# Two stages of a two-block kernel rearranged: the setup with the condition vector first, and the second input projection run together with the lead of the second attention

## The reference, cut to what matters

```python
def first_block(x, c, w_ada, b_ada, ...):
    mod = silu(c) @ w_ada + b_ada                  # six vectors of 1024
    h = rms_norm(x, pre_mix_g) * (1 + sc1) + sh1
    y = token_mixer(h, ...)                        # mLSTM heads and windowed attention, then w_out
    ...                                            # then the conv FFN

def second_block(x, norm1_g, w_in, ...):
    q, k, v, u = split(rmsnorm(x, norm1_g) @ w_in) # 512, 128, 128, 512 columns
    a = attention_mixer(q, k, v)                   # head norm, rope, full attention: 8 heads, 2 key heads
    p = pool_mixer(u)                              # 4 groups: windowed mean minus u, times pool_w, bias, scale
    x = x + concat([a, p]) @ w_out
    ...                                            # then the gated FFN
```

## Time and profile before

| | us |
|---|---|
| median of 3 runs (lowest, highest) | 2560.7 (2559.79, 2563.22) |
| the profiled execution, its own time | 2565.24 |
| its span in the trace | 2563.3 |
| TensorE busy in it | 2409.8 |
| VectorE, ScalarE, GpSimd busy | 1266.6, 832.0, 339.0 |

### The profile page before, as it was taken

The page is one execution under the profiler, slowest core; times in us unless marked ns, Lnnn a source line. Parts: engine busy times, 40 slices in busy tenths (PEclk is TensorE's granted clock), DMA queues, the critical chain, the costliest instruction groups (busy, mean ns, idle before and its releaser), DMA issues. The chain is left out here.

```text
span 2563.3 us, 28634 instructions
## 1 busy us (share of the span) xinstructions
PE 2409.8 (94%) x10895; PEld 1944.7 (76%) x10895; DVE 1266.6 (49%) x1537; ACT 832.0 (32%) x1247; POOL 339.0 (13%) x259
## 2 busy tenths in 40 slices
PE   5999965899999999999998969999999999999998
PEld 4788864677788888888876737777788888888887
DVE  5467246636644444444447359994423333333333
ACT  4232134834422222222235347873321111111111
POOL 1120012413100000000013606651000000000000
PEclk8999987999999999999999989999999999999999
DMA  8146421132211111111123230003111111111111
GB/s 315 57 134 201 143 79 62 33 115 80 60 50 43 48 49 49 49 49 49 50 99 120 58 90 20 22 9 115 34 50 50 49 49 49 49 49 49 49 48 67
DMA packets 188860, 181.92 MB, mean 71 GB/s; under 512 B 8349, under 2 KB 166893, under 8 KB 188145
## 3 DMA queue, kind: packets, MB, share of 16 engines
q1 hardware_dynamic: 185648, 173.36, 21.3%
q0 software_dynamic: 2176, 7.36, 0.9%
q10 hardware_dynamic: 961, 0.18, 0.0%
HBM read 152.55 MB, written 28.33 MB: 71 GB/s over the span
## 5 line engine op out<-in xcount | busy, mean ns | idle before, releaser
L289 PE MATMUL ps<-hhi,whi 128*128 128x512 f32 x1760 | 690.8, 393 | 2.7 <-DVE wlo L215 2.0
L291 PE MATMUL ps<-hhi,wlo 128*128 128x512 f32 x1760 | 686.4, 390 | 0.0
L290 PE MATMUL ps<-hlo,whi 128*128 128x512 f32 x1760 | 686.3, 390 | 0.0
L215 DVE TENSOR_TENSOR wlo<-raw,whi 128x1024 fp32r<-128x1024 f32 x178 | 229.8, 1293 | 369.0 <-ACT whi L210 369.0
L289 PEld LDWEIGHTS ps<-hhi,whi 128*128 128x128 f32 x1760 | 331.5, 188 | 74.3 <-DVE wlo L215 2.4
L290 PEld LDWEIGHTS ps<-hlo,whi 128*128 128x128 f32 x1760 | 331.5, 188 | 70.5 <-issue 1.9
L291 PEld LDWEIGHTS ps<-hhi,wlo 128*128 128x128 f32 x1760 | 331.4, 188 | 69.3
L210 ACT ACTIVATE whi<-raw 128x1024 fp32r<-128x1024 f32 x178 | 184.5, 1049 | 388.0 <-PE ps L2246 286.8
L2397 DVE TENSOR_TENSOR arena<-arena,ps 128x1024 f32<-128x1024 f32 x160 | 195.2, 1220 | 141.1 <-PE ps L2246 140.2
L2244 PE MATMUL ps<-hid_hi,whi 128*128 128x512 f32 x640 | 250.0, 391 | 0.0
L2245 PE MATMUL ps<-hid_lo,whi 128*128 128x512 f32 x640 | 249.2, 389 | 0.0
(11 more groups left out here) (318 smaller groups left out, 3206.7 us busy)
## 6 DMA issues: line engine op xcount, KB each, us to landing
raw<-in_w_up SPq DMA_DIRECT2D x66, 512.0 KB, 3.7
raw<-in_w_down SPq DMA_DIRECT2D x44, 512.0 KB, 3.5
raw<-in_w_in SPq DMA_DIRECT2D x32, 512.0 KB, 5.0
arena<-in_w_ada SPq DMA_DIRECT2D x32, 512.0 KB, 4.7
raw<-in_w_gate SPq DMA_DIRECT2D x22, 512.0 KB, 3.7
raw<-in_w_out SPq DMA_DIRECT2D x16, 512.0 KB, 3.6
arena<-x_park SPq DMA_DIRECT2D x2, 4096.0 KB, 12.2
x_park<-arena SPq DMA_DIRECT2D x4, 2048.0 KB, 8.9
```

What stands on the lines that cost most here:

```text
L215: nc.vector.tensor_tensor(wlo[:, w.off % RING, :], raw[:, w.off % RAW, :], whi[:, w.off % RING, :].bitcast(F32), ALU.subtract).then_inc(lo ...
L289: nc.tensor.matmul(acc[:, tok], whi[:, s, ws], hhi[:, k, tok], start=(k == 0), stop=False)
L290: nc.tensor.matmul(acc[:, tok], whi[:, s, ws], hlo[:, k, tok], start=False, stop=False)
L291: mm = nc.tensor.matmul(acc[:, tok], wlo[:, s, ws], hhi[:, k, tok], start=False, stop=(k == DK - 1))
```

## The change

It has three parts, in one diff.

**Setup.** The condition vector c is loaded by the first DMA of SyncE, and transposed, turned into `csil` before the other parameters are there. The row slots are 13: two of `cbuf`, seven of `chunk_work`, four of the unused halves of `whi` and `wlo`. All 16 rows are queued before the first two weight tiles; the seven small DMAs and the gate columns go behind those, on SyncE. The transposes of x come ahead of those of the parameters. ScalarE loads the table for logarithm and exponential in the setup, and makes the root of x there, beside the second reduction. The split of the gate columns moves behind the operands of the first product.

```diff
-        ada_slots = [cbuf[:, i, :] for i in range(4)] + [chunk_work[:, i * D:(i + 1) * D] for i in range(7)]
+        ada_slots = [cbuf[:, i, :] for i in range(2)] + [chunk_work[:, i * D:(i + 1) * D] for i in range(7)]
+        ada_slots += [v[:, i * D:(i + 1) * D] for v in (row_hi, row_lo) for i in (2, 3)]
...
+                sp.dma_start(c_in, a["c"].rearrange("a (j p) -> (a j) p", p=P)).then_inc(s_c, 16)
...
+                for n in range(ADA_FIRST * DK):
+                    if n >= len(ada_slots):
+                        sp.wait_ge(ada_added, n - len(ada_slots) + 1)
+                    ada_load(n)
+                for w in range(RAW):
+                    load(sp, At(w), tile_source(At(w)))
...
+                for w in range(AHEAD):
+                    split_hi(act, At(w))
+                act.wait_ge(x_summed, 1)
+                norm_mix.act_rstd(act, 0)
```

```diff
-                                mm = nc.tensor.matmul(acc[:, ks], q[:, h // 2, h % 2, :], klo[:, g, ks], start=False,
+                                mm = nc.tensor.matmul(acc[:, ks], q[0:64, h // 2, h % 2, :], klo[0:64, g, ks], start=False,
...
-                                mm = nc.tensor.matmul(o_, v[:, 64:192], ptls[g][:, k, :], start=False,
+                                mm = nc.tensor.matmul(o_[0:64, :], v[:, 64:128], ptls[g][:, k, :], start=False,
...
+                        lead.dve(dve)
                         maxima(At(0), 0)
+                        lead.dve_second(dve)
                         maxima(At(0), 1)
```

```diff
+        def product_by_tiles(pe, acc, w, between, passed=None):
...
+            for k in range(DK):
+                if k in between:
+                    between[k]()
...
+                        between = {2: lambda n=n: self.head_sums(pe, n), 6: lambda n=n: self.rotate(pe, n)}
+                        if t == 9:
+                            between[7] = lambda: self.keys.pe(pe)
...
+            def dve_unit(self, dve, e):
+                if e == 1:
+                    self.rope(dve, 4)
+                if e == 3:
+                    self.query_lo(dve, 3)
...
+            def act_unit(self, act, e):
+                if e == 0:
+                    act.wait_ge(q_lo, 3)
+                    act.wait_ge(q_stored[2], 64)
+                if e == 2:
+                    self.query_hi(act, 3)
+                if e == 4:
+                    act.wait_ge(pooling.mean, 4)
+                    act.wait_ge(q_stored[3], 64)
...
+            def sp_query(self, sp, j):
+
+                if j == 3:
+                    self.store(sp, j)
+                sp.wait_ge(q_stored[j], 64)
...
-                pair_products(pe, w, self.op_lo, u0)
+                pair_products(pe, w, self.op_lo, u0, lambda pe: pooling.pe(pe, range(2)), lambda pe: pooling.pe(pe, range(2, 4)))
```

More of the change, by code:

```diff
@@ L1458, in attention @@
             per_n = 2 * units
[L1459 removed]
+            names = ["keys", "klo", "vturned", "vhi", "vlo", "scores", "stat", "neg_max", "exp", "recip", "scaled",
                      "turned", "p_hi", "p_lo", "pv", "out"]
@@ L1639, in ahead @@
                     def ahead():
-                        nc.scalar.preload_act_table_set(EXP if full else LN_EXP)
+                        lead.act(act)
                         exponentials(At(0), 0)
@@ L1644, in body @@
                         for e in range(per_n):
+                            if full and n.off == 0 and n.i is None:
+                                lead.act_unit(act, e)
                             if e + 1 < per_n or more:
@@ L1698, in body @@
                                                     ALU.mult).then_inc(S["scaled"], 1)
+                            if full and n.off == 0 and n.i is None:
+                                lead.pool_unit(pool, e)
                         if not full and more:
@@ L1852, in body @@
                         for e in range(per_n):
+                            if full and n.off == 0 and n.i is None:
+                                lead.dve_unit(dve, e)
                             if e + 1 < per_n or more:
@@ L2574, in pe, with sums @@
-            def pe(self, pe):
-                for g in range(4):
-                    pe.wait_ge(self.mean, g + 1)
+                        self.link(pool, nc.gpsimd.memset(padded[g][:, side:side + 8], 0.0))
+            def sums(self, pool, g, n):
+                one, two = padded[4], padded[g]
+                pool.wait_ge(self.given, n)
+                if n > 1:
+                    pool.wait_ge(self.mean, n - 1)
+                cur, nxt, span = padded[g], one, PADT
+                for lv in range(g + 1):
+                    d = 1 << lv
+                    span -= d
+                    self.link(pool, nc.gpsimd.tensor_tensor(nxt[:, 0:span], cur[:, 0:span], cur[:, d:d + span], ALU.add))
+                    cur, nxt = nxt, (two if nxt is one else one)
+                return cur[:, 8 - (1 << g):8 - (1 << g) + T], nxt[:, 0:T - 16]
@@ L2577, in pe, with mean_of, difference @@
+            def mean_of(self, pool, g, s, mean):
+                self.link(pool, nc.gpsimd.tensor_scalar(mean, s[:, 8:T - 8], 1.0 / (2 << g), 0.0, ALU.mult, ALU.add))
+            def difference(self, pool, g, mean):
+                u = pool_u[:, g, :]
+                nc.gpsimd.tensor_tensor(u[:, 8:T - 8], mean, u[:, 8:T - 8], ALU.subtract).then_inc(self.mean, 1)
+            def pe(self, pe, gs):
+                for g in gs:
+                    pe.wait_ge(self.mean, 4)
                     if g >= 2:
@@ L2771, in block_kernel, with act @@
-        attention("attn2", True, stage=in2_stage)
+            def act(self, act, g):
+                act.wait_ge(self.product, g + 1)
+                nc.scalar.activation(pool_u[:, g, :], down[g % 2][:, :], ACT.Identity, bias=coef[:, 32 + g:33 + g],
+                                     scale=par_col("pool_scale_2", g)).then_inc(self.biased, 1)
+        pooling = Pooling()
+        ROPED2 = (0, 5, 6, 7, 8)
+        POOLED2 = (2, 3, 4, 9)
+        q_stored = [sem(f"query_stored{j}") for j in range(4)]
@@ L2774, in block_kernel @@
+        attention("attn2", True, SecondInput)
         class Operands:
```

848 lines of the change are left out of this document (427 added, 421 removed).

## The result

The changed kernel takes **2599.7 us** in the median (2596.3 to 2603.5) beside 2560.2 for the kernel before: a ratio of 1.0147, 95% interval 1.0132 to 1.0161. It is 39 us slower, where 30 us were to be gained. The profiled execution took 2602.1 us, its span 2600.3.

The account below looks back on a forecast made before the run. TensorE was busy 94% of the span, so gains could come only where it stands still; VectorE limits the steady full attention. 8.0 + 10.0 + 19.0 − 7.1 = 29.9 us gave 2531 us, range 2521 to 2541.

Parts of the forecast that it names:

- Setup: Start of the kernel: first product at 46.6 instead of 54.66, a gain of 8.0 us, bounds 5.5 and 10.0.
- The mishap of the lower bound: Setup: small DMAs and gate columns hold tile loads, or half clock falls on more square sums; gain only 5.5 us.
- First attention's lead: First attention: queries fetched earlier, so scores start 10.8 us earlier; taken as 10.0 us gain, bounds 8 and 11.5.
- Second projection and attention: Second input projection and full attention: first scaling 29.7 us earlier, part given back; gain 19.0 us, bounds 14 and 23.
- The fourth query: Full attention's first units: its fetch arrives at 1529.1, TensorE wants it at 1525.1; clock restarts cost some 2 us.
- rival 2: Second projection becomes a chain: late norm and root cost 3 us in each of four tiles, 2543 us; chance 0.17.
- Pooling products: Four products move into the second output projection, where TensorE is the bound: 7.1 us paid, bounds 5 and 8.
- the rival with the half-height matmuls: Attentions: height changes not overlapped, 0.17 us each, losing 35 us and up to 28, about 2590; chance 0.07.
- the change of width above: Trace row where width goes from 128 to 64 columns, spacing staying 0.22 us; cited against the half-height rival.

Follow-up runs that it names:

- the kernel with both mends: The changed kernel with low-key matmuls at 128 partitions again in both attentions and the parked x fetched back tile by tile: 2530.8 us, ratio 0.9870.
- the run with half-height products: The kernel before with 84 low-weight matmuls in six tiles of the second input projection cut to 64 partitions: 2599.2 us, ratio 1.0145.
- the kernel before with half height alone: The kernel before with only the low-key matmuls of both attentions cut to 64 partitions: 2621.6 us, ratio 1.0227.

## Why the prediction was wrong

The four terms of the sum held in size; the stages of the kernel with both mends show them without the two disturbances. What failed is what the sum left out.

**Setup**, 8.0: 8.75. The chain came as told, with errors that in part cancel: the third round of transposes stands at 17.9 (forecast 17.0), because x is waited for until 14.8 and not 13; from there to the second reduction it is 20.7 us, not the same 22.6, because the first sums of squares run at the full clock now (1.9 us for four passes, 3.7 before); the first operand operation stands at 41.98 (42.7), the first product at 45.91 (46.6). The mishap of the lower bound did not happen.

**First attention's lead**, 10.0: 10.8 in the mended kernel. The first scores follow the start of the key copies by 5.6 us in the changed kernel (412.12), where it was 16.45: the 10.8 us that the forecast began from. What came behind was slower.

**Second projection and attention**, 19.0: 17.9. The last product's end was put 139.7 us behind the projection's first (1501.1 less 1361.42); in the changed kernel the first scores stood at 1506.4, 139.1 behind. The first scaling came 145.2 us behind (1512.55), forecast 146.1. The fourth query, 4 us and 2 for the clock in the sum, costs 3.2 together. The projection did not become a chain (rival 2): no wait shows inside the tiles t = 6 to 9.

**Pooling products**, 7.1: twice 3.59 us, and the stage grew by 7.7.

The number failed in two places. **First, the rival with the half-height matmuls was priced rightly and given a chance of 0.07, and the sum put them at nothing.** The opening sentence on the long rows of products "that the change leaves as they are" does not hold for the attention, whose matmuls the change reshapes. The rival's 0.7 us per unit is what the timeline shows. Its 35 us for the full attention stand beside 29.8 us lost there; the rows give TensorE 11.5 us free over 56 units, 0.2 each and not 0.15, which makes 32. In the first attention the count was off: a unit has four half-height matmuls, so 8 changes and not 16, and 16 x 8 x 0.17 is 22 us. 24.6 were lost, and these are two things: at full clock a unit takes 5.2 us for 4.1 in the mended kernel, 17 us over 16 units, and the clock, at 0.50 when the scores begin at 412, comes back at 437 in the changed kernel (TensorE waits for nothing in between) and at 417 in the mended one. While it is at 0.50 a change costs more: the starts of a unit's scores lie 0.72 us apart near 1520, where neighbours of one height lie 0.43 apart, so 0.29 us. The rival's 2590 lies only 10 us under the result, and that is in part luck: the doubled count stands in for the late fetch, which it did not have.

The step that failed is the one that set the chance: "Against it: the change of width above". A row that shows a change of width says nothing on one of height; the two turned out opposite. The rule of the Trainium skill (TensorEngine Tiling (Array Packing), section Key Properties), that a change of tiling mode drains the engine, was set aside on that row alone. The runs agree with it for the height, at 0.205 us a change, and not for the width, at 0.005 or less. Rows with a change of height were there, if far from this case: at the gates (L948 and L951, 4 partitions) the loader stands for 0.76 us and then starts together with its matmul, at 153.26. They could not have settled it, because their neighbours are float32 matmuls of four passes, behind which a load also starts with its matmul at equal height (1450.88 and 1450.90 in the run with half-height products); but they left the question open. What would have bound the chance from below was at hand: the full attention gains next to nothing from half height, since VectorE set its pace, so this edit could hardly gain, and its cost was unknown.

How the overlap is lost is shown only as far as the loader's start times go. The Trainium skill (TensorE: Matmul & The Clock Gate, section Step-by-step: what each phase is for) says that a weight load is pulled ahead of running matmuls when row groups do not conflict or when it goes to the background buffer. The traces agree with it at equal heights (the load 0.23 us ahead of its matmul). At a change of height they show no such lead, and the loader idle for 0.24 to 0.37 us. Why was not tried.

**Second, the term of 7.1 us, "The four pooling products move into the second output projection, where TensorE is the bound", took the products' own time and stopped.** The splits of the last four operand tiles were said to be done 1 to 4 us before TensorE asks, and no wait of TensorE for them shows; but TensorE is not the only one to wait for them. SyncE's fetch of the parked x waits for the eighth, and it was moved from 10.1 to 27.7 us into the projection. That opened 9.4 us and the half clock behind it (from 1794.29 to 1799.41 twelve matmuls stand 0.43 us apart for 0.23, 2.4 us): 11.8 of the 12.6 us by which the changed and the mended kernel differ in this stage (20.3 and 7.7). The wait of that queue stood in the code and was not followed.

Forecast 2531, with both mends 2530.8: the sum was right, for a kernel without these two. That the two numbers meet so closely is chance: the kernel before took 2564.4 us beside the mended one, so the gain there is 33 us by the medians and 29.1 by the stages, for a forecast of 29.9.

## What to carry to other kernels

Do not cut a matmul's partitions from 128 to 64 between full ones to save rows of zeros: it makes nothing shorter and costs about 0.2 us at each border; a cut from 128 to 64 columns cost nothing here, and if half height is needed, group it. (Shown for this type of matmul with 256 and 512 moving columns.) When an operation is moved behind another engine's work, list everyone who waits for its last piece, transfers on SyncE's queue first, and ask whether the transfer can leave in pieces. When a rival's mechanism is priced but untested by any row, its chance should not be set by a row that shows something similar, least of all where the edit has no gain to weigh against it.

## What the hardware showed that was not expected

A change of height between two matmuls, 128 to 64 partitions or back, costs 0.205 us in dense products (168 of them, 34.5 us) and 0.17 in the attentions at a granted clock of 1.00, 0.29 at 0.50; a change of width from 128 to 64 columns or back costs at most 0.005 (0.8 us for 168).

The kernels with alternating heights also had the lower clock for longer. In the first attention it is granted at 0.50 until 437 us in the changed kernel and until 417 in the mended one. In the second attention of the kernel before with half height alone it is back at 1581, 23 us after TensorE's last wait; in the kernel before it is back at 1541. The fall to 0.50 for some 7 us near 150 us came within the last 8 of 40 matmuls of 4 and 8 moving columns in six of twelve executions and not in the other six; the stage with it is 4 to 5 us longer. No experiment tried either.
